# A gated convolution with six of its taps on TensorE, full-width taps in two accumulators, and its norm kept in channel layout

## What is computed

```python
h = x @ w_in + b_in                      # 1024 -> 2048: a_val, a_gate, b_gate, b_rec, 512 each
a  = a_val * sigmoid(a_gate)
ya = silu(layer_norm(causal_depthwise_conv(a, conv_w, conv_b), cnorm_g, cnorm_b))   # 31 taps
r  = causal_depthwise_conv(b_rec, lru_conv_w, lru_conv_b)                           # 4 taps
yb = rg_lru(r, ...) * gelu(b_gate)       # gates from r, then a linear recurrence over positions
y  = concatenate([ya, yb], axis=-1) @ w_out
```

## Time and profile before

| | |
|---|---|
| runs | 3891.45 us median of 3 (3887.96 to 3893.44) |
| the profiled execution | 3888.6 us, its span 3886.7 us |
| TensorE matmul busy | 3587.0 us (92%) |
| VectorE busy | 1859.0 us (48%) |
| ScalarE busy | 1218.4 us (31%) |
| POOL busy | 492.2 us (13%) |

### The profile page before, as it was taken

The page is one execution under the profiler, slowest core; times in us unless marked ns, Lnnn a source line. Parts: engine busy times, 40 slices in busy tenths (PEclk is TensorE's granted clock), DMA queues, the critical chain, the costliest instruction groups (busy, mean ns, idle before and its releaser), DMA issues. The chain is left out here.

```text
span 3886.7 us, 41640 instructions
## 1 busy us (share of the span) xinstructions
PE 3587.0 (92%) x15900; PEld 2879.9 (74%) x15900; DVE 1859.0 (48%) x2465; ACT 1218.4 (31%) x1712; POOL 492.2 (13%) x277
## 2 busy tenths in 40 slices
PE   7847999999998989977999999999978889999998
PEld 5636888888876666655888888888866768888886
DVE  7994523223255555545523233554448765322235
ACT  3225521111143333334521111345342343212133
POOL 0003400000061000002400000353001440000004
PEclk9878999999999999978999999999987989999999
DMA  2101213122132111101213123322221222111112
GB/s 92 38 16 65 93 64 108 49 78 84 47 95 62 30 49 32 38 22 54 93 61 108 53 77 108 96 92 93 83 71 39 80 66 92 60 49 49 49 54 98
DMA packets 75997, 261.14 MB, mean 67 GB/s; under 512 B 10224, under 2 KB 10608, under 8 KB 75888
## 3 DMA queue, kind: packets, MB, share of 16 engines
q1 hardware_dynamic: 75888, 259.69, 20.8%
HBM read 246.54 MB, written 4.72 MB: 65 GB/s over the span
## 5 line engine op out<-in xcount | busy, mean ns | idle before, releaser
L197 PE MATMUL ps<-xh,whi 128*128 128x512 f32 x2880 | 1012.4, 396 | 110.0 <-DVE wlo L628 47.4
L197 PE MATMUL ps<-xl,whi 128*128 128x512 f32 x2880 | 1004.1, 393 | 0.0
L197 PE MATMUL ps<-xh,wlo 128*128 128x512 f32 x2880 | 1002.7, 392 | 0.0
L180 DVE TENSOR_TENSOR wlo<-stage,whi 128x1024 fp32r<-128x1024 f32 x366 | 525.4, 1435 | 507.2 <-ACT whi L174 506.1
L174 ACT ACTIVATE whi<-stage 128x1024 fp32r<-128x1024 f32 x366 | 387.0, 1057 | 1099.0 <-PE ps L197 1067.3
L197 PEld LDWEIGHTS ps<-xh,whi 128*128 128x128 f32 x2880 | 546.4, 190 | 237.6 <-issue 86.1
L197 PEld LDWEIGHTS ps<-xh,wlo 128*128 128x128 f32 x2880 | 546.9, 190 | 115.8
L197 PEld LDWEIGHTS ps<-xl,whi 128*128 128x128 f32 x2880 | 547.9, 190 | 112.9
L197 PE MATMUL ps<-hh,whi 128*128 128x512 f32 x1216 | 422.5, 396 | 6.0 <-ACT lam_t L1458 3.9
L197 PE MATMUL ps<-hl,whi 128*128 128x512 f32 x1216 | 421.3, 395 | 0.0
L197 PE MATMUL ps<-hh,wlo 128*128 128x512 f32 x1216 | 421.2, 395 | 0.0
(11 more groups left out here) (324 smaller groups left out, 3757.5 us busy)
## 6 DMA issues: line engine op xcount, KB each, us to landing
stage<-in_w_ff SPq DMA_DIRECT2D x88, 512.0 KB, 3.5
stage<-in_w_gate SPq DMA_DIRECT2D x59, 512.0 KB, 3.3
stage<-in_w_up SPq DMA_DIRECT2D x59, 512.0 KB, 3.3
stage<-in_w_in SPq DMA_DIRECT2D x50, 512.0 KB, 3.2
ada<-in_w_ada SPq DMA_DIRECT2D x48, 512.0 KB, 3.3
stage<-in_w_qkv SPq DMA_DIRECT2D x43, 512.0 KB, 3.3
stage<-in_w_down SPq DMA_DIRECT2D x48, 448.0 KB, 3.3
stage<-in_w_out SPq DMA_DIRECT2D x32, 512.0 KB, 3.3
```

Of the source, the lines that this page charges most:

```text
L180: dve.tensor_tensor(wlo[slot][:], stage[slot][:], whi[slot][:].bitcast(F32), ALU.subtract).then_inc(w_split, 1)
L197: done = pe.matmul(acc[:, h * HALF:(h + 1) * HALF], wt[slot][:, w], xt[:, b, h * HALF:(h + 1) * HALF], start=b == 0 and wt is whi and xt i ...
```

## The change

- In each block of the convolution six taps (25 to 30) become matmuls on TensorE, with a diagonal matrix of the tap's weights and the shifted `a_pad` as data, in fp32, into `ps[2]`, between unit 2 and unit 3 (`taps_of`). ScalarE makes the diagonals from `ident` (`diagonals`).
- The last block does eight more taps so, behind its gates, into `ps[0]`. Its code is written out after a loop over three blocks.
- The other taps on VectorE are one instruction of 1024 positions each, in turn into `conv` and `conv_o`; step 14 adds `ps[2]`, and a last step adds the two accumulators. The LRU taps are full width too, each followed by one step of the convolution.
- All taps stand ahead of the LRU chain. The low half for the next block's unit 2 moves from the start of the next block into the chain, ahead of the scan.
- The norm's program block goes. `ChannelNorm` works in channel layout on halves of 512 positions, inside the block of the out-projection: squares on ScalarE, sums over the four channel blocks on VectorE, totals and broadcast on TensorE, normalising on VectorE, silu and high half on ScalarE, low half on VectorE (first half) and on POOL (second half). The second half is done among units 0 to 4 of `out0a`. POOL's split of `yb` stands at the head of that block.

```diff
@@ -318,91 +318,6 @@
-    def channel_norm(name, src, nblk, gain, bias, dst, other):
...
+    conv_o = sb("conv_o", [P, S], at=lru_scope)
+    PE_TAPS, LATE_TAPS = 6, 8
+    diag = sb("diag", [P, PE_TAPS, P], at=lru_scope)
+    diag_late = w_gates[:].rearrange("p a k n -> p (a k) n")[:, 0:LATE_TAPS, :]
+    diag_ready, tap_mm = ln_stats, ln_aggr
+    a_in = sem("a_in")
+    STEPS = CONV_TAPS - PE_TAPS + 2
+    WITH_PART, SPLIT_AT = 14, 20
+
+    def last_block(i):
+        return isinstance(i, int)
...
+            def taps_of(i, lo, n, w, to):
+                for t in range(n):
+                    for h in range(2):
+                        at = h * HALF + lo + t
+                        done = pe.matmul(to[:, h * HALF:(h + 1) * HALF], w[:, t, :], a_pad[:, at:at + HALF], start=t == 0, stop=t == n - 1)
+                done.then_inc(tap_mm, 1)
+
+            def block_of(i):
+                u = gin0.base + UPB * i
+                mm_unit(pe, gin0, 2 * i, 0, DB, xh, xl, ready)
+                mm_unit(pe, gin0, 2 * i, 1, DB, xh, xl, ready)
+                mm_unit(pe, gin0, 2 * i + 1, 0, DB, xh, xl, ready)
                 pe.wait_ge(gate_w, i + 1)
-                pe.wait_ge(lru_taps, 2 * LRU_TAPS * i + 2 * LRU_TAPS)
+                pe.wait_ge(diag_ready, i + 1)
+                pe.wait_ge(acc_free, u + 4)
+                taps_of(i, CONV_TAPS - PE_TAPS, PE_TAPS, diag, ps[2])
+                mm_unit(pe, gin0, 2 * i + 1, 1, DB, xh, xl, ready)
+                pe.wait_ge(taps, STEPS * i + WITH_PART + 1)
+                pe.wait_ge(lru_taps, LRU_TAPS * i + LRU_TAPS)
                 for k in range(2):
                     for h in range(2):
                         done = pe.matmul(ps[2 + k][:, h * HALF:(h + 1) * HALF], w_now[:, k, :],
                                          rec[:, h * HALF:(h + 1) * HALF], start=True, stop=True)
                 done.then_inc(gate_mm, 1)
+                if last_block(i):
+                    pe.wait_ge(diag_ready, AB + 1)
+                    pe.wait_ge(acc_free, u + 5)
+                    taps_of(i, CONV_TAPS - PE_TAPS - LATE_TAPS, LATE_TAPS, diag_late, ps[0])
...
+            def diagonals(i, lo, n, w):
+                for t in range(n):
+                    done = act.activation(w[:, t, :], ident[:], ACT.Copy, scale=col("conv_w", CONV_TAPS * i + lo + t))
+                done.then_inc(diag_ready, 1)
+
+            diagonals(0, CONV_TAPS - PE_TAPS, PE_TAPS, diag)
...
+                if last_block(i):
+                    act.wait_ge(gate_w, AB)
+                    diagonals(i, CONV_TAPS - PE_TAPS - LATE_TAPS, LATE_TAPS, diag_late)
+                else:
+                    act.wait_ge(tap_mm, i + 1)
+                    diagonals(i + 1, CONV_TAPS - PE_TAPS, PE_TAPS, diag)
...
+            split_lo4(dve, 0, 2)
+
+            def block_of(i):
                 u = gin0.base + UPB * i
-
...
+                out = conv[:, bass.ds(i, 1), :].rearrange("p a n -> p (a n)")
+                n_taps = CONV_TAPS - PE_TAPS - (LATE_TAPS if last_block(i) else 0)
+                step = [0]
+
+                def conv_steps(n):
+                    for _ in range(n):
+                        k = step[0]
+                        t = k if k < WITH_PART else k - 1
+                        dst = conv_o[:] if k % 2 else out
+                        if k == 1:
+                            dve.wait_ge(taps, STEPS * i + 1)
+                        if k >= 2:
+                            dve.wait_ge(taps, STEPS * i + k - 1)
+                        if k == 0:
+                            op = dve.tensor_scalar(dst, a_pad[:, 0:S], col("conv_w", CONV_TAPS * i), col("conv_b", i), ALU.mult, ALU.add)
+                        elif k == 1:
+                            op = dve.tensor_scalar(dst, a_pad[:, 1:1 + S], col("conv_w", CONV_TAPS * i + 1), None, ALU.mult)
+                        elif k == WITH_PART:
+                            dve.wait_ge(tap_mm, i + 1)
+                            op = dve.tensor_tensor(dst, ps[2][:], dst, ALU.add)
+                        else:
+                            op = dve.scalar_tensor_tensor(dst, a_pad[:, t:t + S], col("conv_w", CONV_TAPS * i + t), dst, ALU.mult, ALU.add)
+                        op.then_inc(taps, 1)
+                        step[0] += 1
+
+                def lru_tap(t):
+                    src = r_pad[:, t:t + S]
                     if t == 0:
...
+                        dve.tensor_scalar(rec[:], src, col("lru_w", LRU_TAPS * i), col("lru_b", i), ALU.mult, ALU.add).then_inc(lru_taps, 1)
                     else:
...
-
-                def conv_taps(lo, hi):
-                    for t in range(lo, hi):
-                        for h in range(2):
-                            dst = conv[:, bass.ds(i, 1), h * HALF:(h + 1) * HALF].rearrange("p a n -> p (a n)")
-                            tap(t, h, CONV_TAPS, a_pad, dst, "conv_w", "conv_b", taps)
-
-                split_lo4(dve, i, 2)
+                        dve.wait_ge(lru_taps, LRU_TAPS * i + t)
+                        dve.scalar_tensor_tensor(rec[:], src, col("lru_w", LRU_TAPS * i + t), rec[:], ALU.mult, ALU.add).then_inc(lru_taps, 1)
+
                 dve.wait_ge(mm_done, u + 4)
                 dve.wait_ge(acc_free, u + 3)
                 dve.scalar_tensor_tensor(a_pad[:, PAD_A:], ps[1][:], col("b_in", UPB * i + 1), sig[:],
                                          ALU.add, ALU.mult).then_inc(acc_free, 1)
                 split_lo4(dve, i, 3)
                 dve.wait_ge(acc_free, u + 4)
-                conv_taps(0, TAPS_BEFORE_REC)
+                conv_steps(6)
                 dve.wait_ge(mm_done, u + 5)
                 dve.tensor_scalar(r_pad[:, PAD_R:], ps[0][:], col("b_in", UPB * i + 2), None, ALU.add).then_inc(acc_free, 1)
                 split_lo4(dve, i, 4)
                 dve.wait_ge(acc_free, u + 5)
                 for t in range(LRU_TAPS):
-                    for h in range(2):
-                        tap(t, h, LRU_TAPS, r_pad, rec[:, h * HALF:(h + 1) * HALF], "lru_w", "lru_b", lru_taps)
-                conv_taps(TAPS_BEFORE_REC, TAPS_BEFORE_LRU)
+                    lru_tap(t)
+                    conv_steps(1)
+                conv_steps(min(SPLIT_AT, n_taps + 1) - step[0])
                 split_lo4(dve, i, 5)
-                dve.wait_ge(decays, 2 * i + 2)
+                conv_steps(n_taps + 1 - step[0])
+                done = STEPS * i + n_taps + 1
+                if last_block(i):
+                    dve.wait_ge(decays, 2 * i + 2)
+                else:
+                    dve.wait_ge(taps, done)
+                    dve.tensor_tensor(out, out, conv_o[:], ALU.add).then_inc(taps, 1)
+                    dve.wait_ge(decays, 2 * i + 2)
 
 
                 dve.scalar_tensor_tensor(a_t[:], a_t[:], 1.0, v_t[:], ALU.add, ALU.mult).then_inc(lru_v, 1)
...
                 dve.tensor_tensor(rec[:], rec[:], g_i[:], ALU.mult).then_inc(lru_m, 1)
-                conv_taps(TAPS_BEFORE_LRU, TAPS_BEFORE_SCAN)
+                if last_block(i):
+                    dve.wait_ge(taps, done)
+                    dve.tensor_tensor(out, out, conv_o[:], ALU.add).then_inc(taps, 1)
                 dve.wait_ge(root, i + 1)
                 dve.wait_ge(lru_v, 3 * i + 3)
                 dve.scalar_tensor_tensor(v_t[:], a_t[:], 1.0, v_t[:], ALU.add, ALU.mult).then_inc(lru_m, 1)
                 dve.wait_ge(lru_m, 4 * i + 2)
                 dve.tensor_tensor(rec[:], rec[:], v_t[:], ALU.mult).then_inc(lru_m, 1)
+                if not last_block(i):
+                    split_lo4(dve, i, 6)
                 dve.wait_ge(lru_m, 4 * i + 3)
                 dve.tensor_tensor_scan(v_t[:], a_t[:], rec[:], 0.0, ALU.mult, ALU.add).then_inc(lru_m, 1)
+                if last_block(i):
+                    dve.wait_ge(tap_mm, AB + 1)
+                    dve.wait_ge(taps, done + 1)
+                    dve.tensor_tensor(out, ps[0][:], out, ALU.add).then_inc(taps, 1)
                 dve.wait_ge(lru_m, 4 * i + 4)
                 dve.wait_ge(acc_free, u + 6)
                 dve.tensor_tensor(yb[:, bass.ds(i, 1), :].rearrange("p a n -> p (a n)"), v_t[:], gel[:], ALU.mult).then_inc(lru_u, 1)
-                conv_taps(TAPS_BEFORE_SCAN, CONV_TAPS)
-                dve.wait_ge(taps, 2 * CONV_TAPS * i + 2 * CONV_TAPS)
...
-    channel_norm("cnorm", conv, AB, lambda b: col("cnorm_g", b), lambda b: col("cnorm_b", b), conv, yb)
     conv_scope.close()
+    c_sq = at_kb("c_sq", [P, AB, S], 32)
+    c_sum = at_kb("c_sum", [P, 2, 2, HALF], 48)
...
+
+        def squares(self, act):
+            for b in range(AB):
+                act.activation(c_sq[:, b, self.t], conv[:, b, self.t], ACT.Square).then_inc(cn_sq, 1)
+
+        def sums(self, dve):
+            h = self.h
+            for b in range(1, AB):
+                for q, src in enumerate((conv, c_sq)):
+                    to = c_sum[:, h, q, :]
+                    if q:
+                        dve.wait_ge(cn_sq, AB * h + b + 1)
```

(108 more changed lines are left out.)

165 lines of the change are left out of this document (72 added, 93 removed).

## The result

The changed kernel takes 3852.16 us, the median of four runs (3844.92 to 3856.19); the kernel before, on the same chip, 3892.44 (3887.96 to 3904.46). The ratio is 0.989, 95% interval 0.9863 to 0.9916: 40.3 us less, well clear of no change. The forecast was 3844 us, with a likeliest case from 3836 to 3851 and a range from 3832 to 3861. The profiled execution took 3844.92 us; it is the fastest of the four.

The account below looks back on a forecast made before the run. VectorE bounded the convolution and ScalarE the norm after it, with TensorE waiting on both. 3888.6 less 29.5 (convolution) less 15.3 (norm) gave 3844 us, range 3832 to 3861.

Parts of the forecast that it names:

- rival 1: Convolution: VectorE stays the bound, taps at 1.34 and longer round trips, 61.4 us a block against 57.2; 3857 us; chance 0.14.
- rival 2: Norm: a chain of semaphores, half the expected gain plus 5 us wait for late POOL; 3857 us; chance 0.14.
- TensorE's block: Convolution, TensorE's time per block: units 43.5, gate matmuls 3.4, six diagonal taps 10.3, sum 57.2 us; becomes the bound.
- Rival 3: Convolution: fp32 diagonal passes get the low clock, 0.855 us a pass, adding 65 us; 3909 us; chance 0.04.
- VectorE's block: Convolution, VectorE's time per block: 52.1 us of work, 54.7 with waits for ScalarE and the loop turn.
- wait (a): Convolution, VectorE's split for unit 5 after 20 steps: waits 1.0 us for ScalarE's high half.
- (b): Convolution, VectorE's moved split of unit 6: waits 1.0 us for ScalarE's sqrt, sigmoid and copy.
- End of the convolution: Last block's end, after the LRU chain and late taps: 261.7 us instead of 291.2, a gain of 29.5.
- The norm: From the convolution's end to unit 1 of `out0a`: 28.6 us against 43.9, a gain of 15.3.
- The block change: Start of the norm, from the convolution's end: 0.5 us for changing program block.

Follow-up runs that it names:

- run 7: Changed kernel with eight taps a block on TensorE instead of six; 3870.01 us.
- run 8: Changed kernel with five taps a block on TensorE instead of six; 3843.83 us.
- run 5: Changed kernel with no taps on TensorE, all 31 full-width on VectorE in two accumulators; 3864.55 us.
- run 1: Changed kernel with POOL's four low halves of `yb` held until VectorE's twelve sums of the norm are done; 3857.8 us.
- run 10: Changed kernel with POOL's four 1024-wide subtractions on `yb` cut into eight of 512; 3847.66 us.
- run 9: Changed kernel with POOL's subtractions on `yb` held until the first half's reciprocal deviation is there; 3840.65 us.
- run 4: Changed kernel with each convolution tap on VectorE as two half-width instructions into one accumulator, six taps still on TensorE; 3854.89 us.
- run 6: Changed kernel with the low half for unit 2 back at the start of the block, ahead of `a_pad`; 3858.26 us.
- run 12: The changed kernel itself, unedited, timed again beside the kernel before; 3859.5 us, ratio 0.9897.

## Why the prediction was right

The result, 3852, is 8 us above the predicted time and inside the range, but 1 us above the likeliest case (3836 to 3851). By the number alone it lies nearer to the 3857 of rivals 1 and 2 than to 3844. What makes the forecast right is its mechanism, which the dates of the steps show:

- **TensorE's block**, 57.2 predicted, 57.3 measured. 24 diagonal passes take 10.47, the last one's passage included, where 10.3 was said. Runs 7 and 8 moved the number of taps, and the period followed by 1.7 us a tap, up to 60.75 and down to 55.6. Rival 3, the low clock, did not come: the granted clock of the stage is 1.00.
- **VectorE's block**, 54.7 predicted, 54.9 measured (57.3 less the idle of 1.95 and 0.50 that it spends on TensorE). `r_pad` has an idle of 1.95 (said: some 2); a tap holds the engine for about 1.2 at full width, tap 1 with its odd start is fast (0.75). Waits (a) and (b) were put at 1.0 each and are 1.22 and 0.80, in sum 2.0. By the Trainium skill's 1380 ns drain (ScalarE: Activation LUTs, "What ACT_TABLE_LOAD costs") they would have been 1.4 longer each, an estimate; the trace does not agree. In run 8 one tap more didn't lengthen VectorE's block (55.6 less 0.95 is 54.7): the tap filled wait (a), which is gone there. Rival 1's 61.4 was not reached; only run 5, without any tap on TensorE, comes there (60.5 to 61.4).
- **End of the convolution**, 261.7 predicted, 260.3 measured: gain 30.9 instead of 29.5.
- **The norm is the step that was mis-sized.** From the convolution's end to the start of unit 1 28.6 were predicted, 33.8 measured (260.30 to 294.05): a gain of 10 instead of 15.3. The term is "12 half-width sums on VectorE, 0.6 each alone and 1.0 each beside POOL ...: 10.2". They take 16.5 (261.33 to 277.83), 6.3 more, four of them at 2.8. The block change took 1.0 instead of 0.5. The rest up to unit 1 took 16.2, where its terms add up to 17.4; the second half's broadcast was counted in them and stands behind unit 1 (299.63). The terms of the whole sum add up to 28.1, not 28.6: a slip of 0.5.
- Why 1.0: it scaled the 1.99 that a 1024-wide split took beside POOL with the width. The row was one instruction that met POOL's for a part of its length. The trace of the kernel before has this one beside it:

```profile
374.15 1.29 POOL L459 TENSOR_TENSOR sum_a<-sum_a,x 128x512 f32<-128x512 f32 x1 [1.92 <-DVE x L586]
```

It ends at 375.44, 0.9 after the split's start, and the split's excess is 0.8: a remainder of waiting and no rate. Runs 1 and 10 show that: the excess follows POOL's instruction (2.15 and 1.07 for 1024 and 512 columns) and is 2.0 to 2.1 even where VectorE's own work is 0.16. The Trainium skill has the rule (SBUF — State Buffer, "SBUF: two separate sides"): the port pair shared by the two is "an exclusive lock, not a bandwidth split", held for a whole instruction. By the same page ("Who interferes with whom") a VectorE instruction with two SBUF inputs contends, and one with at most one SBUF input, outside the two-port modes, doesn't. The runs agree where both inputs are in SBUF (sums at 2.8, two small steps at 2.18 and 2.26) and where one is in PSUM (1.22 beside POOL, run 9). For L828, with its one tensor, the rule holds only if it ran in a two-port mode, which no run shows. Without the rule, rows 3 have the price: POOL's four instructions take 9.29, and if the sums wait for all of it they need 12 x 0.6 + 9.3 = 16.5 instead of 10.2. That is what they took, and the forecast would have been 3850.
- **Rival 2** came near the loss in the norm (7.7 us of the gain, 5.2 measured) with the wrong cause: the hand-overs went as priced, and TensorE waits for nothing from 292 to 420 us, so not for POOL's sums for `mix0[0]` either.
- **The profiled execution** agrees with the 3844 more closely (3844.92) than the dates do: 3.9 us late at unit 1, 2.7 given back by a shorter rest that no step of the sum foresaw. That agreement is luck; the same program's rest was 20 us longer in another execution. The medians are the fairer comparison: 40.3 us less, where the steps gave 44.8; the dates say 40.9.

## What to carry to other kernels

When two engines share a stage, price the one that the change makes the bound, move work one unit at a time until the other has no slack left (runs 7 and 8), and expect that speeding up the other is worth nothing (runs 4 and 6). Before work of VectorE on SBUF operands is put beside POOL's, lay the two timelines side by side: each such instruction, however small, waited for the POOL instruction under way in these runs, so start POOL behind the latency chain, beside steps that read PSUM. And when a row shows an instruction slowed by a neighbour, ask whether the excess is a rate or a wait before scaling it.

## What was not expected of the hardware

- A VectorE step on 128 x 4 numbers took 2.18 to 2.27 us beside POOL and 0.16 alone (run 1).
- Behind the norm, TensorE's clock differs between nearly equal kernels. In the changed kernel units 0 and 1 of `out0a` are evicted 7.3 us apart, in runs 1 and 7 10.3 apart. Between 290 and 300 us the granted clock was 0.91 in the changed kernel, 1.00 in its second execution (run 12) and 0.65 in run 1. In run 1 the second half's totals took:

```profile
290.49 3.41 PE L815 MATMUL ps<-share,c_sum 128*128 128x2 f32 x16
```

against 1.84. That cost run 1 the 1.8 us that it had gained up to unit 0 (290.73 against 292.55), and 1.2 more. TensorE had waited 3.2 us for a low half (L869) in unit 0 there, 1.8 in the changed kernel; but in run 6 it waited 3.1 and its units are 7.2 apart, so what decides it is open.
- With diagonal passes where TensorE had waited, the granted clock of the whole convolution stage is 1.00; before it was 0.85, and 0.87 in run 5 without diagonals (20 to 276 us). No run separates what that alone is worth.
